# Three edits in one kernel: substitution on VectorE in the RWKV stage, new slots in the delta stage, scaled exponentials in the attentions

## The chip, the cores and the metric

One core of a Trainium2 chip runs a whole two-block network in one launch, all in 32-bit floats. The metric is the device time of one execution in microseconds, median of three.

## The reference, cut to what matters

512 tokens of width 1024 pass an RWKV-7 mixing layer, an MLP, a forgetting attention, an MLP, and then a second block: gated delta rule in both directions, latent attention (MLA), and an expert-choice MLP. Three places matter here.

```python
# RWKV-7: 16 heads of 64; the kernel works it in chunks of 64 tokens
S = S * w_t[:, :, None, :] + sa[..., :, None] * b_t[..., None, :] + v_t[..., :, None] * k_t[..., None, :]
# delta rule: 8 heads of 128, two directions, chunks of 64
t_inv = lax.linalg.triangular_solve(eye + lower, ..., left_side=True, lower=True, unit_diagonal=True)
# both attentions, in blocks of 128 queries
p = jax.nn.softmax(s, axis=-1)
return jnp.einsum('bhqk,bhkd->bhqd', p, v)
```

In both recurrences each chunk needs the inverse of a unit triangular 64x64 matrix. Both attentions need the weights p normalised, and turned, since TensorE sums over partitions.

## The kernel before, in words

**Slots and rounds.** Five engine programs are written as streams that yield at slot ends. `rounds` weaves, in each of 12 rounds, five stages of five neighbouring items: chain, scores, post, prep, fetch (this order in each slot). An item is a pair of heads `ct` in RWKV (8 items, 24 slots) and a head `hd` with both directions in delta (8 items, 32 slots). A slot fixes the order of instructions in each engine's own queue; between engines only semaphores order. So in slot n every engine does what its streams put there, and whoever is behind makes the others wait. Rounds 0 to 7 hold the projections (`pe_fetch`, four 128x512 products in slots 2, 5, 8, 11, 14 and 17 of RWKV; `pe_dfetch`, in every fourth slot of delta). Later rounds don't.

**The chain.** `pe_chain` walks eight chunks, three slots each: xs, then uu, then the new state's part `ds` and the output y. ScalarE copies xs and uu in between, VectorE adds the state (`dv_chain`, 128x64). Delta's chain has four slots per chunk.

**The inverse.** `pe_scores` makes an upward series of levels 0 to 5 with blocks of 2, 4, ... 64. Each level takes groups of 16 products of 64x64 (8 chunks, two halves; a 32-bit product is two instructions in the trace): u, then t and tt, with VectorE masking u to `A_` and copying tt to `TT`, and ScalarE copying t to `T_`. In RWKV all six levels are done so. In delta (`pe_dscores`, `dv_dscores`) levels 1 to 3 are already replaced: VectorE turns the diagonal 16x16 blocks out of the scores by 32x32 stream transposes, substitutes them column by column (`solve16`, two dependent small instructions for each j from 1 to 14), ScalarE and GpSimd spread the result back into blocks, two stream transposes return it, and TensorE does levels 4 and 5.

**The attentions.** Forgetting attention runs 40 units (8 pairs of heads, five units each, of 512 score columns in all: two whole block rows, two split 384+128, one 256+256). For a unit TensorE scores, VectorE takes the maximum (`dv_max`), ScalarE exponentiates with the sum on the side, VectorE takes the reciprocal and writes identity times reciprocal (`dv_diagonal`), TensorE multiplies each 128x128 block of exponentials by that diagonal, which turns and scales it (`pe_weights`), ScalarE copies, TensorE multiplies with the values. Unit n + 2 is scored before unit n is turned. Latent attention does the same in 16 steps of two heads (`pe_heads`, `dv_lmax`, `LDG`); in steps 0 to 2 of each four TensorE has other products between scores and weights, in step 3 they lie ahead of the scores.

In the profile almost all instructions have the line of a helper: L79 is a product, L82 a transpose on TensorE, L70 a VectorE or GpSimd operation of two tensors, L73 one with scalars, L76 the fused one, L87 a ScalarE activation.

Of the kernel before, what the change touches and what calls it, by code (L numbers as in the profile page):

```python
# [10 lines left out]
P = 128  # L11
# [130 lines left out]
def consts():  # L142
# [30 lines left out]
    for n in range(2):  # L173
        f[:, 68 + n] = np.arange(128) % 4 == np.arange(128) % 64 // 32 * 2 + n
    out["d_tri"] = np.concatenate([both(jj <= ii, jj >= ii), -1.0 * both(jj < ii, jj > ii)], axis=1)
# [45 lines left out]
def program(nc, a, out):  # L221

    ctx = ExitStack()
    with ctx:
# [31 lines left out]
        x3, h3 = kt(X[:, :]), kt(H[:, :])  # L256

# [506 lines left out]
        T_, A_ = c8(cv(512)), c8(cv(512))  # L764
# [20 lines left out]
        def bank8(b):  # L785
            return c8(BK[b][:, :])
# [193 lines left out]
        def pe_scores(pe, ct, left):  # L980
# [36 lines left out]
            pe.wait_ge(s_gp, ngp["m", ct])  # L1017
            for c in range(8):
                for h in half:
                    m = pe.mm(bank8(4)[h, c, :], m8[h, c, :], rcon("r64", rows=h), True, True)  # L1020
            m.then_inc(s_pe, npe("u", ct, 0))
# [5 lines left out]
            for lev in range(1, 6):  # L1027
                x, y = (5, 4) if lev % 2 else (4, 5)
                if lev == 1:
                    pe.wait_ge(s_dv, ndv["t", ct, 0])  # L1030
                    each(x, m8, T_).then_inc(s_pe, npe("u", ct, lev))
                yield
                if lev == 1:
                    pe.wait_ge(s_gp, ngp["tt0", ct])
                else:
                    pe.wait_ge(s_dv, ndv["tt", ct, lev - 1])
                pe.wait_ge(s_dv, ndv["a", ct, lev])
                if lev < 5:
                    each(y, TT, A_).then_inc(s_pe, npe("t", ct, lev))
                each(x, A_, TT).then_inc(s_pe, npe("tt", ct, lev))  # L1040
                yield
                for n, (src, b) in enumerate(((V, 2), (c8(KH), 2), (c8(BH), 3))):
                    if lev == 1 + n:
                        pe.wait_ge(*((s_gp, ngp["end", ct, n - 1]) if n else (s_ac, nac["v", ct])))
                        pe.wait_ge(*left[b])
                        turn(src, b).then_inc(s_pe, npe("tok", ct, n))
                        left[b] = (s_ac, nac["tok", ct, n])
                if lev < 5:
                    pe.wait_ge(s_ac, nac["t", ct, lev])
                    each(y, m8, T_).then_inc(s_pe, npe("u", ct, lev + 1))  # L1050
                yield
            yield from idle(4)

        def gp_scores(gp, ct):
# [3 lines left out]
            gp.wait_ge(s_dv, ndv["sb", ct, 1])  # L1058
            gp.tt(m8, m8, over8("r64", 0), ADD).then_inc(s_gp, ngp("m", ct))
            gp.wait_ge(s_gp, ngp.n)  # L1060
            if ct >= 2:
                gp.wait_ge(s_pe, npe["headed", ct - 2])
            gp.tt(TTs[ct % 2], m8, over8("r64", 64), MUL).then_inc(s_gp, ngp("tt0", ct))
# [6 lines left out]
            yield from idle(17)  # L1070

        def ac_scores(ac, ct):
            yield from idle(5)
            if ct >= 2:
                ac.wait_ge(s_pe, npe["headed", ct - 2])
            for lev in range(1, 6):
                yield
                if lev < 5:
                    ac.wait_ge(s_pe, npe["t", ct, lev])
                    ac.act(T_, bank8(4 if lev % 2 else 5), COPY).then_inc(s_ac, nac("t", ct, lev))  # L1080
                yield
                for n, (dst, b) in enumerate(((Vts[ct % 2], 2), (KHts[ct % 2], 2), (BHts[ct % 2], 3))):
                    if lev == 1 + n:
                        ac.wait_ge(s_pe, npe["tok", ct, n])
                        ac.act(dst, bank8(b), COPY).then_inc(s_ac, nac("tok", ct, n))
                yield
            yield from idle(4)

        def dv_scores(dv, ct):
# [13 lines left out]
            masked("sb", NRs[ct % 2], 5, 1)  # L1103
            yield
            yield
            masked("sk", AKs[ct % 2], 2, 0)
# [2587 lines left out]
```

## Time and profile before

| | us |
|---|---|
| three runs, median (lowest to highest) | 3521.67 (3516.02 to 3525.56) |
| the profiled execution | 3509.0 |
| its span, first to last instruction | 3507.2 |
| RWKV's rounds, about | 120 to 600 |
| forgetting attention's units, about | 1320 to 1430 |
| delta's rounds, about | 1905 to 2500 |
| latent attention's steps, about | 2660 to 2850 |

The tile names are: A the big arena in SBUF, SM, X, H and W other SBUF areas, con the constants, bank a PSUM bank. PE is TensorE's products, PEld its weight loads, DVE VectorE, ACT ScalarE, POOL GpSimd. "Idle before" is what the engine waited just before the instruction, and the arrow names what ended that. A run of small products on TensorE is shown with the last one's latency (0.2 to 0.3 us), so times per product are read from start to start.

### The profile page before, as it was taken

How to read it: one execution, taken by the hardware profiler on the slowest of the kernel's cores; microseconds unless marked ns; L12 is line 12 of the kernel's file. 1: busy time of each engine (PE TensorE's matmuls, PEld its weight loads, DVE VectorE, ACT ScalarE, POOL GpSimd, SP SyncE). 2: the span in 40 equal slices, each digit the busy share in tenths (PEclk: the TensorE clock that was granted, in tenths of full speed). 3: DMA queues.
4: the chain of work that ended last, by engine and by line, in shares of the span. 5: the costliest groups of instructions: out<-in, count | busy, mean ns of one | idle time of the engine just before them, and what ended most of it. 6: DMA issues, size and time to landing. Idle time of an engine off the chain costs nothing.

```text
span 3507.2 us, 51167 instructions
## 1 busy us (share of the span) xinstructions
PE 3350.6 (96%) x22310; PEld 2162.8 (62%) x22310; DVE 1580.3 (45%) x2993; ACT 761.7 (22%) x1580; POOL 379.4 (11%) x298
## 2 busy tenths in 40 slices
PE   8999998999999999999999899998999999899999
PEld 3566666888884657788887454554445656434343
DVE  4454553788743225688832666555212204201011
ACT  2323332211003025311001333233222320211111
POOL 0010110233001000122100211212100001000000
PEclk9999998999999999999999999998999999899999
DMA  5321202255651220156622111100221114699997
GB/s 198 121 74 46 87 7 78 80 180 180 204 157 61 72 77 9 49 156 187 185 84 74 48 37 26 36 25 1 58 66 43 48 44 150 248 421 421 421 421 284
DMA packets 355791, 452.81 MB, mean 129 GB/s; under 512 B 25712, under 2 KB 282992, under 8 KB 331760
## 3 DMA queue, kind: packets, MB, share of 16 engines
q1 hardware_dynamic: 355568, 449.55, 37.4%
q8 instruction: 175, 2.87, 0.3%
q14 instruction: 48, 0.39, 0.0%
HBM read 445.27 MB, written 4.20 MB: 128 GB/s over the span
## 4 chain that ended last, share of the span: by engine, by line
PE 85%; DVE 8%; DMA 3%; ACT 3%; issue 1%; POOL 0%; SPq 0%; POOLq 0%; DVEq 0%; ACTq 0%
PE bank L79 84%; DVE A L70 2%; DVE A L76 2%; DMA A<-in_w_up 2%; ACT A L87 1%; DMA W<-in_w_up 1%; DVE A L73 1%; PE bank L82 0%; POOL A L73 0%; DVE H L70 0%; ACT SM L87 0%; DVE SM L76 0%; DVE X L76 0%; DMA A<-in_x 0%; ACT H L87 0%
## 5 line engine op out<-in xcount | busy, mean ns | idle before, releaser
L79 PE MATMUL bank<-A 64*64 64x64 f32 (+6 forms) x11424 | 1004.2, 271 | 59.9 <-ACT A L87 27.8
L79 PEld LDWEIGHTS bank<-A 64*64 64x64 f32 (+3 forms) x11424 | 785.8, 152 | 322.7 <-issue 117.9
L79 PE MATMUL bank<-A,W 128*128 128x256 f32 (+1 forms) x2240 | 719.0, 475 | 2.9 <-DMA W<-in_rw_g 1.6
L79 PE MATMUL bank<-H,W 128*128 128x512 f32 (+2 forms) x1712 | 644.4, 526 | 24.8 <-ACT H L87 14.4
L79 PEld LDWEIGHTS bank<-A,W 128*128 128x128 f32 x2240 | 417.8, 191 | 253.9 <-issue 213.0
L87 ACT ACTIVATE A<-bank 128x64 f32<-128x64 f32 (+4 forms) x493 | 208.6, 427 | 1434.6 <-PE bank L79 1339.7
L79 PEld LDWEIGHTS bank<-H,W 128*128 128x128 f32 (+1 forms) x1712 | 316.5, 192 | 289.3 <-issue 257.5
L79 PE MATMUL bank<-A,H 128*64 128x512 f32 (+2 forms) x1224 | 309.6, 572 | 6.1 <-DMA A<-in_w_up 3.3
L70 DVE TENSOR_TENSOR A<-bank,A 128x256 f32<-128x256 f32 (+1 forms) x350 | 157.9, 462 | 178.1 <-PE bank L79 158.9
L70 POOL TENSOR_TENSOR A<-A 128x512 f32<-128x512 f32 (+1 forms) x103 | 145.6, 1420 | 749.6 <-ACT A L87 389.6
L87 ACT ACTIVATE A<-A 128x512 f32<-128x512 f32 (+1 forms) x238 | 138.0, 610 | 398.8 <-DVE A L70 368.5
L79 PEld LDWEIGHTS bank<-A,H 128*64 128x64 f32 (+1 forms) x1224 | 113.9, 145 | 171.6 <-issue 150.5
L79 PE MATMUL bank<-W,H 128*64 128x512 f32 (+3 forms) x952 | 208.9, 476 | 0.0
L76 DVE SCALAR_TENSOR_TENSOR SM<-W,cact,SM 128x512 f32<-128x512 f32 x206 | 188.4, 914 | 9.3
L70 DVE TENSOR_TENSOR A<-W 128x512 f32<-128x512 f32 x152 | 107.4, 747 | 176.6 <-PE bank L79 87.7
L70 DVE TENSOR_TENSOR A<-bank,SM 128x512 f32<-128x512 f32 x16 | 10.3, 686 | 344.8 <-PE bank L79 344.8
L79 PEld LDWEIGHTS bank<-W,H 128*64 128x64 f32 (+1 forms) x952 | 85.7, 159 | 101.0 <-issue 100.6
L70 DVE TENSOR_TENSOR A<-A 128x50 f32<-128x50 f32 (+9 forms) x282 | 106.5, 379 | 58.0 <-ACT A L87 49.3
L70 POOL TENSOR_TENSOR SM<-SM 128x512 f32<-128x512 f32 x31 | 41.2, 1330 | 817.5 <-ACT SM L87 815.2
L76 DVE SCALAR_TENSOR_TENSOR X<-bank,mods,X 128x256 f32<-128x256 f32 (+1 forms) x144 | 86.7, 603 | 89.7 <-PE bank L79 84.1
L79 PE MATMUL bank<-A,con 128*128 128x512 f32 (+2 forms) x174 | 92.8, 658 | 24.1 <-ACT A L87 12.2
L79 PE MATMUL bank<-H,A 128*128 128x256 f32 x448 | 107.4, 381 | 0.0
(185 smaller groups left out, 2576.5 us busy)
## 6 DMA issues: line engine op xcount, KB each, us to landing
A<-in_w_gate SPq DMA_DIRECT2D x47, 1024.0 KB, 22.4
W<-in_mod_w SPq DMA_DIRECT2D x45, 1024.0 KB, 7.3
A<-in_w_up SPq DMA_DIRECT2D x42, 1024.0 KB, 19.3
A<-in_w_down SPq DMA_DIRECT2D x35, 1024.0 KB, 27.0
W<-in_mlp_up SPq DMA_DIRECT2D x64, 512.0 KB, 5.4
W<-in_mlp_down SPq DMA_DIRECT2D x128, 256.0 KB, 4.0
W<-in_w_mod SPq DMA_DIRECT2D x24, 1024.0 KB, 5.4
W<-in_w_up SPq DMA_DIRECT2D x22, 1024.0 KB, 19.0
```

Of the source, the lines that this page charges most:

```text
L70: return self.e.tensor_tensor(o, x, y, op)
L73: return self.e.tensor_scalar(o, x, s1, s2, op0, op1) if op1 is not None else self.e.tensor_scalar(o, x, s1, None, op0)
L76: return self.e.scalar_tensor_tensor(out=o, in0=x, scalar=s, in1=y, op0=op0, op1=op1, **kw)
L79: return self.e.matmul(o, l, r, start=start, stop=stop, skip_group_check=True)
L87: return self.e.activation(o, i, func, bias=bias, scale=scale)
```

## The change

**RWKV.** The same VectorE substitution comes into `pe_scores` and its companions. TensorE's groups u0 to u3, t1 to t3 and tt1 to tt3 go; u4, t4, tt4, u5 and tt5 stay, now in slots 16, 18, 18, 19 and 21 (before 13, 15, 15, 16 and 18). VectorE adds a stream transpose in slot 1, two parity passes, a fill of ones, steps j = 1 to 14 in slots 2 to 13, and two stream transposes in slot 15, which wait for the spreads by ScalarE and GpSimd in slot 14. It drops its masks t0 and a1 to a3 and its copies tt1 to tt3. GpSimd's first TT goes, one spread comes.

**Delta.** The steps take one slot each (3 to 16; before 3 to 13, some doubled). GpSimd's spread is one masked two-tensor instruction per half (two in all, slot 17) where there were four scalar ones (slot 14); ScalarE's four stay and move from slot 14 to 17; the stream transposes move from slot 15 to 19; level 4 from slots 17 and 18 to 22 and 23, level 5 from 21 and 22 to 26 and 27. The turns of values and keys stay in slots 12, 16, 20 and 24.

**Attentions.** The diagonals go. VectorE multiplies the exponentials in place by the reciprocal, and TensorE transposes the blocks against the identity. Latent attention's `LDG` also waited for the last step's product; that wait goes.

```diff
@@ pe_scores, RWKV
-            pe.wait_ge(s_gp, ngp["m", ct])
-            for c in range(8):
-                for h in half:
-                    m = pe.mm(bank8(4)[h, c, :], m8[h, c, :], rcon("r64", rows=h), True, True)
-            m.then_inc(s_pe, npe("u", ct, 0))
...
-            for lev in range(1, 6):
+            for lev in range(4, 6):
                 x, y = (5, 4) if lev % 2 else (4, 5)
-                if lev == 1:
-                    pe.wait_ge(s_dv, ndv["t", ct, 0])
-                    each(x, m8, T_).then_inc(s_pe, npe("u", ct, lev))
+                if lev == 4:
+                    pe.wait_ge(s_gp, ngp["m", ct])
+                    pe.wait_ge(s_dv, ndv["t", ct, 3])
...
@@ gp_scores
-            gp.tt(TTs[ct % 2], m8, over8("r64", 64), MUL).then_inc(s_gp, ngp("tt0", ct))
...
+            gp.wait_ge(s_dv, ndv["inv", ct])
+            spread16(gp, AM, XI).then_inc(s_gp, ngp("ett", ct))
@@ ac_scores
+            ac.wait_ge(s_dv, ndv["inv", ct])
+            for n in range(2):
+                m = ac.act(of16(TTf)[:, :, 16 * n:16 * n + 16], XI.rearrange("p i c -> p c i"), COPY, scale=parity(n))
@@ dv_scores
+            dv.e.transpose(of16(AM), by16(NRs[ct % 2][:, :, 0, :])).then_inc(s_dv, ndv("raw", ct))
+            yield
+            dv.wait_ge(s_dv, ndv.n)
+            dv.ts(XI, of16(AM)[:, :, 0:16], parity(0), None, MUL, None).then_inc(s_dv, ndv())
+            dv.wait_ge(s_dv, ndv.n)
+            dv.stt(XI, of16(AM)[:, :, 16:32], parity(1), XI, MUL, ADD).then_inc(s_dv, ndv())
...
+            for j in range(1, 15):
+                if j not in (1, 8, 12):
+                    yield
...
+                solve16(dv, XI, XTMP, j).then_inc(s_dv, ndv() if j < 14 else ndv("inv", ct))
+            yield
+            yield
+            dv.wait_ge(s_ac, nac["et", ct])
+            dv.wait_ge(s_gp, ngp["ett", ct])
+            dv.e.transpose(by16(T_), of16(TT.rearrange("p c t -> p (c t)"))).then_inc(s_dv, ndv("t", ct, 3))
+            dv.wait_ge(s_dv, ndv.n)
+            dv.e.transpose(by16(TT), of16(AM)).then_inc(s_dv, ndv("tt", ct, 3))
@@ helper, and its use in gp_dscores
+        def spread16(e, st, x, rows=slice(0, P)):
+            n = rows.stop - rows.start
+            mask = C("iota")[rows, 68:70].unsqueeze(1).unsqueeze(3).broadcast_to([n, 16, 2, 16])
+            return e.tt(st.rearrange("p (c q j) -> p c q j", q=2, j=16), x.unsqueeze(2).broadcast_to([n, 16, 2, 16]), mask, MUL)
...
-            for n in range(2):
-                for h, i in zip(half, ("p i c -> p i c", "p i c -> p c i")):
-                    gp.wait_ge(s_gp, ngp.n)
-                    m = gp.ts(of16(DAM)[h, :, 16 * n:16 * n + 16], DXI[h, :, :].rearrange(i), parity(n, h), None, MUL, None)
+            for h, i in zip(half, ("p i c -> p i c", "p i c -> p c i")):
+                gp.wait_ge(s_gp, ngp.n)
+                m = spread16(gp, DAM[h, :], DXI[h, :, :].rearrange(i), h)
@@ dv_dscores
-                if j in (1, 3, 4, 5, 6, 7, 9, 10, 11, 12, 13):
-                    yield
+                yield
                 solve16(dv, DXI, DXTMP, j).then_inc(s_dv, ndv() if j < 14 else ndv("dinv", hd))
@@ pe_weights and dv_diagonal, forgetting attention
-                    m = pe.mm(b[:, c], Eu[n % 4][:, c], DGu[n % 4][i], True, True)
+                    m = pe.tr(b[:, c], Eu[n % 4][:, c], C("ident"))
...
-                m = dv.ts(DGu[n % 4][i], C("ident"), s[:, 4 * i + 2:4 * i + 3], None, MUL, None)
+                e = Eu[n % 4][:, o:o + 128 * qt + 128]
+                m = dv.ts(e, e, s[:, 4 * i + 2:4 * i + 3], None, MUL, None)
@@ pe_heads and dv_lmax, latent attention
-                        m = pe.mm(BK[2 + e][:, s], LE[e][:, s], LDG[e], True, True)
+                        m = pe.tr(BK[2 + e][:, s], LE[e][:, s], C("ident"))
...
-                if n:
-                    dv.wait_ge(s_pe, npe["lp", n - 1, e])
-                dv.ts(LDG[e], C("ident"), lsm[e][:, 3:4], None, MUL, None).then_inc(s_dv, ndv("ldg", n, e))
+                dv.ts(LE[e], LE[e], lsm[e][:, 3:4], None, MUL, None).then_inc(s_dv, ndv("ldg", n, e))
```

## Rows read from the trace of the kernel before

**Rows 1.** The page: span, and busy time, share and instructions by engine.
```profile
span 3507.2 us, 51167 instructions
...
PE 3350.6 (96%) x22310; PEld 2162.8 (62%) x22310; DVE 1580.3 (45%) x2993; ACT 761.7 (22%) x1580; POOL 379.4 (11%) x298
```
**Rows 2.** Busy times by stretch, RWKV: a full round, the two without projections.
```profile
core 0: us, PE busy (x) PEld busy (x) DVE busy (x) ACT busy (x) POOL busy (x), PEclk, DMA share, GB/s
430.60:491.90 61.30, 59.60 (x958) 39.96 (x955) 30.47 (x56) 19.54 (x45) 6.91 (x5) 1.00 0.14 46
491.90:533.80 41.90, 39.17 (x910) 31.52 (x908) 25.80 (x48) 17.96 (x42) 6.36 (x5) 1.00 0.02 5
533.80:567.00 33.20, 31.66 (x770) 27.25 (x768) 12.93 (x23) 9.71 (x24) 4.58 (x4) 0.95 0.10 31
```
**Rows 3.** The same for delta: a full round, the first without projections.
```profile
2226.80:2295.40 68.60, 62.20 (x509) 34.80 (x508) 40.85 (x98) 21.40 (x43) 11.59 (x10) 0.95 0.10 31
2363.80:2413.80 50.00, 38.01 (x442) 26.24 (x438) 30.96 (x84) 18.94 (x38) 7.70 (x7) 0.83 0.01 1
```
**Rows 4.** Timeline of RWKV, TensorE: start, length, then [idle before and releaser].
```profile
433.48 0.33 PE L79 MATMUL bank<-A 64*64 64x64 f32 x4
...
434.13 0.68 PE L79 MATMUL bank<-A 64*64 64x64 f32 x16 [0.32 <-ACT A L87]
...
460.67 1.10 PE L79 MATMUL bank<-W,X 64*64 64x64 f32 x32
461.60 1.57 PE L79 MATMUL bank<-A 64*64 64x64 f32 x48
```
**Rows 5.** Timeline of one full delta round, three places.
```profile
2245.34 1.27 POOL L70 TENSOR_TENSOR A<-A,con 128x512 f32<-128x512 f32 x1
2245.45 1.22 DVE L70 TENSOR_TENSOR A<-A 128x50 f32<-128x50 f32 x1
...
2253.01 0.66 PE L79 MATMUL bank<-A 128*64 128x128 f32 x8 [1.01 <-DVE A L76]
...
2259.50 4.94 POOL L73 TENSOR_SCALAR A<-A,con 64x256 f32<-64x256 f32 x4 [12.89 <-DVE A L70]
...
2264.55 1.06 DVE L2458 STREAM_TRANSPOSE A<-A 128x512 f32<-128x512 f32 x1 [3.65 <-POOL A L73]
```
**Rows 6.** Timeline of the forgetting attention (maxima), and of a latent step's weights.
```profile
1358.40 0.69 DVE L1978 TENSOR_REDUCE A<-bank 128x1 f32<-128x512 f32 x1 [0.32 <-PE bank L79]
...
1360.38 0.69 DVE L1978 TENSOR_REDUCE A<-bank 128x1 f32<-128x512 f32 x1
...
1366.80 0.76 DVE L1978 TENSOR_REDUCE A<-bank 128x1 f32<-128x384 f32 x2 [0.41 <-PE bank L79]
...
1369.30 0.75 DVE L1978 TENSOR_REDUCE A<-bank 128x1 f32<-128x256 f32 x2
...
1372.19 0.69 DVE L1978 TENSOR_REDUCE A<-bank 128x1 f32<-128x512 f32 x1 [0.32 <-PE bank L79]
...
2752.08 2.05 PE L79 MATMUL bank<-A,SM 128*128 128x128 f32 x16 [0.31 <-DVE A L73]
```
**Rows 7.** VectorE's groups by shape: busy us, mean ns, idle before.
```profile
L70 DVE TENSOR_TENSOR A<-bank,W 128x512 f32<-128x512 f32 x80 | 54.5, 684 | 47.1 <-PE bank L79 46.6
...
L2440 DVE STREAM_TRANSPOSE A<-A 128x512 f32<-128x512 f32 x8 | 8.4, 1053 | 0.3
...
L70 DVE TENSOR_TENSOR A<-A 128x56 f32<-128x56 f32 x32 | 6.9, 217 | 1.1
```
**Rows 8.** Busy times of two stretches at the start, where TensorE only transposes.
```profile
11.30:14.80 3.50, 3.46 (x17) 3.50 (x18) 0.00 (x0) 2.28 (x4) 0.00 (x0) 1.00 1.05 390
14.90:16.60 1.70, 1.70 (x17) 1.60 (x15) 0.00 (x0) 1.70 (x4) 0.00 (x0) 1.00 1.05 387
```
**Rows 9.** VectorE's scalar operations of line 73: ns min/median/max, first and last start.
```profile
L73 DVE TENSOR_SCALAR A<-con,A x96: 278/286/290, 1321.4 to 2845.3; 128x128 f32<-128x128 f32 x96
...
L73 DVE TENSOR_SCALAR A<-SM,cols x24: 476/478/1182, 1932.9 to 2350.8; 128x512 f32<-128x512 f32 x24
```

More of the change, by code:

```diff
@@ L1041, in pe_scores @@
                 yield
[L1042 to L1050, printed above, removed]
-                yield
-            yield from idle(4)
+            yield from idle(2)
         def gp_scores(gp, ct):
@@ L1069, in gp_scores @@
                 yield
-            yield from idle(17)
+            yield from idle(7)
+            gp.wait_ge(s_dv, ndv["inv", ct])
+            spread16(gp, AM, XI).then_inc(s_gp, ngp("ett", ct))
+            yield from idle(10)
         def ac_scores(ac, ct):
+            TTf = TTs[ct % 2].rearrange("p c t -> p (c t)")
             yield from idle(5)
@@ L1122, in dv_scores @@
                 yield
-            yield from idle(4)
+            yield
         def pe_chain(pe, ct):
@@ L1704, in program @@
         PTu = [HQ[:, 2048 + 512 * n:2560 + 512 * n] for n in range(4)]
-        DGu = [[cv(128) for _ in range(2)] for _ in range(4)]
         smu = [cv(8) for _ in range(4)]
@@ L2387, in pe_dscores, with tokens @@
-            yield from idle(7)
+            def tokens(n):
+                b = 1 + n % 2
+                pe.wait_ge(*left[b])
+                turn(vf if n < 2 else QK[:, :, 0, :], b, n % 2).then_inc(s_pe, npe("dtok", hd, n))
+                left[b] = (s_ac, nac["dtok", hd, n]) if n < 2 else (s_dv, ndv["dtok", hd, n])
+            yield from idle(12)
+            tokens(0)
+            yield from idle(4)
+            tokens(1)
+            yield from idle(4)
+            tokens(2)
+            yield from idle(2)
@@ new lines, in pe_dscores @@
+            pe.wait_ge(s_gp, ngp["dm", hd])
+            pe.wait_ge(s_dv, ndv["dt", hd, 3])
+            each(3, m8, DT).then_inc(s_pe, npe("du", hd, 4))
+            yield
+            pe.wait_ge(s_dv, ndv["dtt", hd, 3])
+            pe.wait_ge(s_dv, ndv["da", hd, 4])
+            each(4, TT, DA).then_inc(s_pe, npe("dt", hd, 4))
+            each(3, DA, TT).then_inc(s_pe, npe("dtt", hd, 4))
+            yield
+            tokens(3)
+            yield from idle(2)
+            pe.wait_ge(s_ac, nac["dt", hd, 4])
@@ L2488, in pe_dchain @@
+            yield
+            dv.wait_ge(s_pe, npe["dtt", hd, 5])
+            dv.e.tensor_copy(TT, bank8(4)).then_inc(s_dv, ndv("dtt", hd, 5))
+            yield from idle(5)
         def pe_dchain(pe, hd):
@@ L2719, in program @@
         QR = [cv(512) for _ in range(2)]
-        LDG = [cv(128) for _ in range(2)]
         lsm = [cv(8) for _ in range(2)]
```

198 lines of the change are left out of this document (96 added, 102 removed).

## The prediction

> **What bounds the kernel now.** I read the page first. TensorE is busy for 96% of the span, VectorE for 45%, and the granted clock in the rounds quoted below is between 0.83 and 1.00 [rows 1 to 3]. So what matters is TensorE's own work, and where it pauses. Then the busy times by stretch. One full round of the first mixing stage (RWKV; 24 slots) takes 61.3 us with TensorE busy for 59.60 and VectorE for 30.47; the two rounds without projections take 41.9 and 33.2 us [rows 2]. A full round of the delta stage (32 slots) takes 68.6 us, and its first round without projections 50.0 us at clock 0.83 [rows 3]. Last the timeline. A light slot of the RWKV chain is bare waiting: 0.32 us shown for ScalarE's copy [rows 4], and from issue to issue 0.65 us (433.48 to 434.13) where the four instructions fill 0.12, so some 0.5 us. In delta, TensorE waits 1.01 us for a state update that stands behind VectorE's queue, and VectorE itself waits 3.65 us for GpSimd's spreads [rows 5]. The forgetting attention is TensorE-bound, 1372.19 - 1358.40 = 13.79 us per pair of heads, with a second loop close behind (below) [rows 6].
>
> **Part A, RWKV.** Per pair of heads (8 of them) ten groups of 16 64x64 products go: u0 to u3, t1 to t3, tt1 to tt3. A group is 32 instructions on TensorE and takes 461.60 - 460.67 = 0.93 us [rows 4]. 10 x 0.93 x 8 = **74.4 us** of work that lies on the path.
>
> Given back, per full round:
> - Slots that lose their filler. The chain goes product, ScalarE copy, product, ScalarE copy, product, VectorE update, in slots 3c, 3c+1, 3c+2. Before, the bare slots are 1, 19, 20, 21 and 22; after, 1, 3, 6, 9, 15, 20 and 22. Two more at 0.5: **1.0 us**.
> - The end. Level 5's product moves from slot 18 to 21, where only light slots lie ahead: it waits for VectorE's masking, 0.68 us (the first row of [rows 7]), and the next round for its copy: **0.8 us**.
> - VectorE. It loses seven passes of 0.68 (t0, a1 to a3, tt1 to tt3), 4.8 us. It gains 28 substitution instructions of at most 0.217 (the smaller ones less), some 5.7 us, three stream transposes of 1.053, and two parity passes, nearest row 0.478 [rows 9]: 9.8 us ([rows 7] for the rest). Besides, a two-input VectorE instruction that meets a GpSimd one stands still: 1.22 us for one of 50 columns [rows 5], where 56 take 0.217 [rows 7]. GpSimd has five instructions per round (6.91 us) [rows 2], of which some four now meet substitution steps: 4 us. So VectorE has 30.5 - 4.8 + 9.8 + 4 = 40 us in a round of some 54: it doesn't bound, but its order shows. Bounds for what TensorE sees of it: nothing (3.4 us of projection hide every update in slots 2 to 17), or 1.01 us [rows 5] at each of 7 updates. I take **1.0**, nearer to the lower end, for that cover.
>
> - The added waits. In slot 15 VectorE waits for the spreads of slot 14. GpSimd's takes about 1.27 us (nearest row) [rows 5]; behind the wait stand t0 of the bonus and the update of slot 17, and TensorE's u4 waits for it in slot 16. Slot 14 holds 3.4 us of projection, so a full round pays **nothing**; a round without projections pays up to 1.3 us, which is in the 4 us below. In slot 14 ScalarE waits for the last substitution step; behind it stands the copy of xs, again with the projection as cover.
>
> The Trainium skill says of that standstill (SBUF — State Buffer, on the port pair that VectorE and GpSimd share) that it is an exclusive lock, held for the whole instruction. The 1.22 us agrees; the sum above goes by the row.
>
> So a full round, or one that is nearly full (six of them), gives 9.3 - 2.8 = 6.5 us: 39 us. In the two rounds without projections VectorE's 25.80 and 12.93 us [rows 2] become some 33 and 20 with many waits between, and a slot is shorter than a step and an update together; I take 4 us each, between 0 and 9.3: 8 us. A thinner TensorE there will also drop its clock more often: 0.95 now [rows 2], 0.83 in the like round of delta [rows 3], over some 60 us: between 0 and 7, I take 5. **A: 39 + 8 - 5 = 42 us**, between 20 and 68.
>
> **Part B, delta's slots.** No product goes. VectorE's steps are one per slot (before, two or three in slots 3, 8 and 13), so the update waits shrink by one step, 0.43 us, at two or three places of a round: 1.2 us in five full rounds, 6 us. GpSimd's four spreads (4.94 us) [rows 5] become two; the nearest row for one is 1.27 us, so 2.5 us, and three slots lie ahead of the wait instead of one. In a full round that wait hides behind projections; in the first one and in the first without projections it doesn't: some 3 us each, 6. The products of levels 4 and 5 leave slots 17 and 21, where they hid a ScalarE copy (two more bare, 0.5 each) for 22, 23, 26 and 27, where they hide the update (two less): nothing. The clock of 0.95 and 0.83 [rows 3] may recover a little: 3 us. **B: 15 us**, between -5 (the late levels come too late for the next round) and 28.
>
> **Part C, attentions.** 160 + 128 products of a 128x128 block by a diagonal become transposes. A product is two instructions; 16 of them take 2.05 us with the tail of the last [rows 6], some 0.11 each, so 0.22 a block. A transpose is one instruction: the same tile size has 17 in 3.50 us at the start, then 17 in 1.70 us [rows 8], at most 0.11. That saves 0.11 a block: 17.6 and 14.1 us on TensorE.
>
> VectorE now scales up to 512 columns instead of a 128-column diagonal. 128 take 0.286, 512 with a column of scalars 0.478 [rows 9]: +0.19 for one block row, about +0.15 for the split units.
> - Forgetting attention. max, exp, reciprocal, scaling, next max is a loop of its own: 1360.38 - 1358.40 = 1.98 us for a whole unit, 1369.30 - 1366.80 = 2.50 for a split one (both maxima started without a wait for TensorE) [rows 6]. Per pair of heads 2 x 2.17 + 3 x 2.65 = 12.3 us after, against TensorE's 13.79 - 20 x 0.11 = 11.6. The loop becomes the bound: 1.5 us for each of eight, less 1 for the sums of the next product that VectorE does beside the last ones: **11 us**, between 5 and 17.6.
> - Latent attention. Twelve of 16 steps have projections between scores and weights and give 0.88 each. The other four wait for the scaling already (0.31 shown) [rows 6] and give some 0.35: **12 us**, between 9 and 14.
>
> The Trainium skill (TensorE: Matmul & The Clock Gate, "Part 4: PE-mode transpose") says that a transpose doesn't count as activity for the clock gate. This trace speaks against it: 17 instructions take 3.50 us, 0.21 each, and the next 17, from 14.90 us on, 1.70 us, 0.10 each [rows 8]. That is the lower clock (1.2 GHz) and then 2.4 GHz, though the clock column, which has no record that early, says 1.00 for both, and TensorE did nothing but transposes between.
>
> **The sum.** 42 + 15 + 23 = 80 us. The profiled execution has 3509.0 us (span 3507.2), so 3429; the median of the three timed runs is 12.7 higher, so **3441.7 us**.
>
> **Rivals.**
> 1. TensorE stays the bound everywhere, and the queues hide what I deduct: 74.4 + 31.7 + 20 = 126 us, 3396. For it: 96% busy [rows 1], and VectorE below 50% in RWKV. Against: the loop of 1.98 and 2.50 us. 15%.
> 2. VectorE's order eats part of it: RWKV gives only 15 to 20 us, attention's ends stay. 3521.7 - 18 - 10 - 20 = 3474. For it: the 1.01 us in the stage that already works this way. 16%.
> 3. Slower: the state update of RWKV always stands behind a locked substitution step. Price per update 1.01 for the queue and 1.0 for the lock [rows 5], 56 updates: 112 us, of which 6 are in my sum: 3548 us. It decides from 1.5 us per update on. Against: 3.4 us of projection follow most updates before anyone needs them. 5%.
> 4. The transposes don't hold the clock. The nearest row for a stretch that drops often is 0.83 [rows 3]; over the 300 us of the two attentions that is 60 us: 3502. 2%. The page named above would have it so; [rows 8] doesn't.
> 5. The diagonal doesn't really cost two instructions, or a transpose is no cheaper in place: part C gives 0, 3465. 4%.
>
> **How the numbers follow.** My forecast has 58%. The range from 3392 to 3482 leaves out the further half of rival 1, rivals 3 and 4, and a few mishaps: under 2 in 10. Faster by over 0.3% (about 10 us, what a measurement of this kernel can tell from no change): forecast, rivals 1, 2, 4 and 5, less mishaps, 93%. Within: 3%. Slower: 4%.
>
> **What would show it.** Right: RWKV full rounds of some 54 to 55 us with VectorE near 37; 64x64 products fewer by 2560 instructions; delta's wait for GpSimd under 1 us and rounds of 67 us; maxima of the forgetting attention 2.2 and 2.65 us apart with TensorE idle for up to a tenth; latent steps shorter by 0.9. Wrong: TensorE's waits for VectorE's 128x64 updates over 1 us in RWKV, a granted clock under 0.9 there, or delta rounds longer than 69 us.

## The result and the profile after

The changed kernel takes 3468.97 us, the kernel before, timed beside it, 3523.61 (four runs each): ratio 0.985, 95% interval 0.983 to 0.987, **55 us less**. The prediction said 3441.7, with a range from 3392 to 3482. The total lies in the range, but the prediction had taken off 80 us where 55 came, and by stages it is another sum: the delta stage, put at 15 us shorter, got longer. The profiled execution takes 3460.95 us, 48 less than that of before.

The page of the changed kernel (span; busy us, share and instructions by engine). TensorE has 22310 - 19462 = 2848 instructions less: the 2560 of the RWKV products and 288 of the diagonals. VectorE has 64 us more:
```profile
span 3459.2 us, 45630 instructions
...
PE 3257.4 (94%) x19462; PEld 2062.2 (60%) x19462; DVE 1644.2 (48%) x3209; ACT 754.4 (22%) x1572; POOL 363.0 (10%) x282
```
Busy times by stretch, changed kernel (columns as in [rows 2]): two full RWKV rounds, the two rounds without projections, a full delta round and the first one without projections. They answer [rows 2, 3]:
```profile
342.70:400.10 57.40, 51.65 (x638) 31.15 (x636) 36.98 (x84) 19.00 (x44) 6.54 (x5) 1.00 0.22 67
400.10:458.40 58.30, 54.33 (x638) 32.92 (x636) 35.81 (x84) 18.88 (x44) 7.03 (x5) 0.94 0.13 42
458.40:499.70 41.30, 32.89 (x590) 23.80 (x588) 31.59 (x77) 17.22 (x41) 6.54 (x5) 0.92 0.02 6
499.70:530.00 30.30, 24.33 (x488) 19.20 (x486) 20.26 (x52) 9.50 (x25) 4.35 (x4) 0.94 0.31 101
2252.50:2321.50 69.00, 60.73 (x519) 34.54 (x519) 42.41 (x99) 21.15 (x43) 9.46 (x8) 0.98 0.07 20
2321.50:2368.50 47.00, 35.49 (x440) 23.86 (x438) 29.96 (x83) 18.87 (x38) 5.91 (x5) 0.89 0.01 2
```
A full RWKV round fell from 61.3 us to 57.4 and 58.3, not to 54 or 55. A full delta round didn't fall at all (68.1 to 68.7 us before, 68.7 to 70.7 after). The rows of before show two of its four full RWKV rounds; the other two were longer, at a lower granted clock:
```profile
240.80:304.30 63.50, 61.80 (x958) 42.04 (x956) 31.25 (x56) 19.54 (x45) 6.89 (x5) 0.96 0.15 43
304.30:369.30 65.00, 61.66 (x959) 41.77 (x958) 30.98 (x56) 19.55 (x45) 6.89 (x5) 0.97 0.18 56
```
From round to round, before: 49.1, 57.2, 63.5, 65.0, 61.3, 61.3, 41.9 and 33.2 us. Changed: 42.7, 49.9, 56.6, 58.6, 57.4, 58.3, 41.3 and 30.3. The gains are 6.4, 7.3, 6.9, 6.4, 3.9, 3.0, 0.6 and 2.9.

To follow each stage from kernel to kernel I use marks that all have: the starts of RWKV's rounds (first product of the bonus), the reciprocals of both attentions, and the first stream transpose of each delta round. The list of one line's instructions gives the ends of the last two (ns min/median/max, first and last start), here for the delta transpose, the forgetting attention's and the latent one's reciprocal. Kernel before:
```profile
L2440 DVE STREAM_TRANSPOSE A<-A x8: 1047/1052/1064, 1979.4 to 2413.8; 128x512 f32<-128x512 f32 x8
L1986 DVE RECIPROCAL A<-A x64: 142/164/166, 1321.2 to 1426.8; 128x1 f32<-128x1 f32 x64
L3060 DVE RECIPROCAL A<-A x32: 162/164/166, 2661.4 to 2845.1; 128x1 f32<-128x1 f32 x32
```
Changed kernel:
```profile
L2481 DVE STREAM_TRANSPOSE A<-A x8: 1040/1051/1065, 1934.4 to 2368.5; 128x512 f32<-128x512 f32 x8
L2031 DVE RECIPROCAL A<-A x64: 143/164/165, 1282.8 to 1384.3; 128x1 f32<-128x1 f32 x64
L3101 DVE RECIPROCAL A<-A x32: 163/164/165, 2624.6 to 2798.1; 128x1 f32<-128x1 f32 x32
```
- Up to the first reciprocal of the forgetting attention: 1321.2 - 1282.8 = 38.4 us gained (part A).
- Forgetting attention, first to last reciprocal: 105.6 to 101.5, 4.1 gained. Between it and delta another 2.5.
- Delta, from its first transpose to the latent attention's first reciprocal: 682.0 to 690.2, **8.2 lost** (part B, predicted as a gain of 15). Between the first and the last of the transposes nothing changed (434.4 and 434.1); the loss lies behind the last.
- Latent attention, first to last reciprocal: 183.7 to 173.5, 10.2 gained.

Three things stand out in the changed kernel's trace. In RWKV (TensorE; start, length, [idle before and releaser]) the bare slot is as in [rows 4], but a wait for weights is new:
```profile
425.51 0.33 PE L79 MATMUL bank<-A 64*64 64x64 f32 x4 [0.32 <-ACT A L87]
...
433.41 1.23 PE L79 MATMUL bank<-A,W 128*128 128x512 f32 x2 [1.80 <-DMA W<-in_rw_g]
```
Between 134 and 560 us TensorE waits four times for these weights, 7.2 us in all; before, once, 1.6 us. They are the gate's weights, the fifth load of a round on a ring with four slots: they get the slot of the k and r weights, which comes free at order slot 11, and are used in slot 12. By the order of the slots, the product work that stood in slots 10 to 12 had hidden part of the load, and the change took it out.

In a full delta round (TensorE and VectorE; it answers [rows 5]):
```profile
2268.92 1.27 POOL L70 TENSOR_TENSOR A<-A,con 128x512 f32<-128x512 f32 x1
2269.04 2.33 DVE L70 TENSOR_TENSOR A<-A 128x44 f32<-128x44 f32 x2
...
2275.32 0.86 PE L79 MATMUL bank<-A 64*128 64x128 f32 x8 [0.81 <-ACT A L87]
...
2277.46 1.12 PE L79 MATMUL bank<-A 128*64 128x128 f32 x8 [1.28 <-DVE A L76]
...
2287.99 3.71 POOL L70 TENSOR_TENSOR A<-A,con 64x512 f32<-64x512 f32 x3 [15.33 <-DVE A L70]
...
2294.51 1.05 DVE L2497 STREAM_TRANSPOSE A<-A 128x512 f32<-128x512 f32 x1 [0.29 <-ACT A L87]
...
2299.20 1.79 PE L79 MATMUL bank<-A 64*128 64x128 f32 x40 [0.38 <-ACT A L87]
2301.78 2.67 PE L79 MATMUL bank<-A 64*64 64x64 f32 x72 [0.79 <-DVE A L70]
...
2309.69 1.79 PE L79 MATMUL bank<-A 64*128 64x128 f32 x40 [0.38 <-ACT A L87]
2312.28 1.74 PE L79 MATMUL bank<-A 64*64 64x64 f32 x40 [0.79 <-DVE A L70]
```
VectorE's wait for the spreads did go (3.65 to 0.29 us), but nobody on TensorE was waiting for it. Instead levels 4 and 5 have moved to where ScalarE's copy and VectorE's masking of u lie open, 0.38 and 0.79 twice each.

Still, what the five rounds from the second to the sixth lost (5.6 us), the first (50.2 to 47.2) and the first without projections (50.0 to 47.1) gave back. The stage's net loss is in the round after these, the second without projections (cut at TensorE's 32 products `bank<-con,A 64*128 64x64`, early in each round). Before, then changed:
```profile
2414.38:2474.71 60.33, 56.43 (x467) 29.23 (x465) 24.85 (x75) 14.15 (x30) 27.80 (x21) 0.94 0.01 1
```
```profile
2369.13:2437.95 68.82, 59.65 (x467) 30.64 (x465) 27.50 (x75) 14.26 (x30) 26.16 (x19) 0.90 0.00 1
```
TensorE's shown waits there are 9.2 us instead of 4.0. GpSimd's long run of other work on X, which stood behind the spreads (from 2445.3 us, 31 us into the round), now starts at 2371.0, 2 us into it, beside VectorE's first steps: two of VectorE's parity passes take 2.31 us together instead of 1.16, and a wait of TensorE for VectorE right after is 2.6 instead of 0.8. A wait of 2.3 for a ScalarE copy, which stands behind the four moved spreads, is new. The granted clock is 0.90 instead of 0.94.

### The profile page after: what moved, and what is told of

Same layout as the page of the kernel before. It is cut to its first block, busy times and chain, and to the rows that moved or that the text cites. A ratio compares the mean times of both kernels' runs of the same rounds, so it can differ in the third digit from the quotient of the medians.

```text
span 3459.2 us, 45630 instructions
## 1 busy us (share of the span) xinstructions
PE 3257.4 (94%) x19462; PEld 2062.2 (60%) x19462; DVE 1644.2 (48%) x3209; ACT 754.4 (22%) x1572; POOL 363.0 (10%) x282
## 4 chain that ended last, share of the span: by engine, by line
PE 82%; DVE 9%; ACT 4%; DMA 4%; issue 1%; SPq 0%; POOLq 0%; POOL 0%; DVEq 0%; ACTq 0%
PE bank L79 82%; DVE A L70 2%; DMA A<-in_w_up 2%; DVE A L76 2%; ACT A L87 2%; DVE A L73 1%; PE bank L82 1%; ACT A L86 1%; DMA W<-in_w_up 1%; DVE A L2023 1%; DMA W<-in_mod_w 1%; DVE H L70 0%; ACT SM L87 0%; DVE X L76 0%; DMA A<-in_x 0%
## 5 line engine op out<-in xcount | busy, mean ns | idle before, releaser
L79 PE MATMUL bank<-A 64*64 64x64 f32 (+6 forms) x8800 | 904.3, 286 | 97.9 <-ACT A L87 49.9
L79 PEld LDWEIGHTS bank<-A 64*64 64x64 f32 (+3 forms) x8800 | 684.4, 156 | 365.2 <-issue 99.2
L87 ACT ACTIVATE A<-bank 128x512 f32<-128x512 f32 (+4 forms) x469 | 193.8, 418 | 1377.9 <-PE bank L79 1333.4
L70 DVE TENSOR_TENSOR A<-A 128x14 f32<-128x14 f32 (+9 forms) x506 | 160.9, 320 | 65.7 <-ACT A L87 49.2
L79 PE MATMUL bank<-A,con 128*128 128x512 f32 (+2 forms) x174 | 88.8, 634 | 22.0 <-ACT A L87 12.3
```

Source lines behind the costliest of these rows:

```text
L70: return self.e.tensor_tensor(o, x, y, op)
L79: return self.e.matmul(o, l, r, start=start, stop=stop, skip_group_check=True)
L87: return self.e.activation(o, i, func, bias=bias, scale=scale)
```

## The experiments

Every kernel was timed beside the kernel before on its own chip; ratios are to that, with 95% intervals.

### One part at a time

**RWKV alone.** The kernel before with this and the rest of the first mixing stage's part of the diff:
```diff
-            for lev in range(1, 6):
+            for lev in range(4, 6):
```


> The RWKV part of the change alone (the substitution on VectorE in the first mixing stage), with delta rounds and attentions as before. Theory, from the round starts of the two traces: 38 us shorter than before, about 3484 us, with the delta stage's first to last stream transpose at 467 us and the time between reciprocals in the forgetting attention at 105.6 us, both as before. The prediction on record gave this part 42 us (3480). Rival, that the parts help or hurt one another through what they prefetch across the stage borders: the sum of the three parts alone differs from 54.6 us by more than 5.

3472.31 us against 3518.56, ratio 0.987 (0.986 to 0.988): **46 us** shorter; its round starts run from 140.3 to 503.9, 363.6 us where before has 399.3. The other two kernels that keep the old RWKV take 401.8 and 405.1, so the profiled execution of before stood at the low end, and the part may be worth more than the 38 read first. The prediction's 42 lies at the edge of the timed interval (42 to 51).

**Delta alone.**
```diff
-                if j in (1, 3, 4, 5, 6, 7, 9, 10, 11, 12, 13):
-                    yield
+                yield
                 solve16(dv, DXI, DXTMP, j)...
```


> The new slots of the delta rounds alone. Theory, from the two traces: 7 to 8 us longer than before, about 3530 us, with rounds that have projections of 69 to 70 us instead of 68.3. The prediction on record: 15 us shorter, 3508, rounds of 67. Rival: the slots are worth nothing by themselves and what the trace of after showed is one execution's scatter, within 3 us of before.

3530.10 against 3518.56, ratio 1.0034 (1.0022 to 1.0046): **12 us longer**. First transpose to the latent attention's first reciprocal: 691.8 us against 682.0; the second round without projections takes 67.6 us (60.3 before). The sign of part B was wrong, by itself as well as inside the change.

**Attentions alone.**
```diff
-                    m = pe.mm(b[:, c], Eu[n % 4][:, c], DGu[n % 4][i], True, True)
+                    m = pe.tr(b[:, c], Eu[n % 4][:, c], C("ident"))
```


> The attentions' part alone (exponentials scaled on VectorE, then turned). Theory, from the two traces: forgetting attention 6.6 us and latent attention 10.2 us shorter, 17 us together, about 3506 us. The prediction on record: 11 and 12, 23 us, 3500. Rival, that the forgetting attention gains nothing and the latent one all that is seen: 10 us.

3501.53, ratio 0.9956 (0.994 to 0.997): 17 us shorter. The trace has 2.7 us of it in the forgetting attention (105.6 to 102.9) and 10.0 in the latent one. Its profiled execution was the longest of the seven (3514.6), so only the stage lengths are read from it, not its total; where the other 4 us lie isn't shown.

**The change without its delta part** (all slots and spreads of the delta rounds as before):

```diff
 # against the changed kernel
             for j in range(1, 15):
-                yield
+                if j in (1, 3, 4, 5, 6, 7, 9, 10, 11, 12, 13):
+                    yield
```


> The change without its delta part: delta rounds as before, RWKV and attentions as changed. Theory: the delta part costs 7 to 8 us inside the change, so this runs 62 us under before, about 3461 us, and beats the changed kernel by 7. The prediction on record, by which the delta part saves 15 us: 40 us under before, about 3484. Rival, no effect of the delta part: 55 us under before, 3469.

3461.88, ratio 0.9836 (0.982 to 0.985), 57 us shorter: so less than 46 + 17, by some 7. Against the changed kernel's 0.985 (0.986 in a repetition below) it is 5 to 9 us ahead, though the intervals meet. The single parts are nearly, not exactly, additive.

### What costs delta its sign

**Levels one slot earlier.** Products, ScalarE copy and VectorE maskings of levels 4 and 5 move from slots 22, 23, 26, 27 to 21, 22, 25, 26, the same places between the chain's products as the old 17, 18, 21, 22:
```diff
             tokens(2)
-            yield from idle(2)
+            yield
             pe.wait_ge(s_gp, ngp["dm", hd])
...
-            yield
+            yield from idle(2)
             tokens(3)
-            yield from idle(2)
+            yield
             pe.wait_ge(s_ac, nac["dt", hd, 4])
```


> The changed kernel with the delta rounds' levels 4 and 5 one slot earlier, so that their products stand again in the same places between the chain's products as before the change, and everything else of the new slots kept (substitution one step per slot, one spread instruction per half, spreads at slot 17). Theory, that the places of the levels cost the delta part its sign (two more bare waits for ScalarE of 0.5 us and two maskings of 0.8 in the open per full round): rounds with projections fall from 69.5 to 67.5 us, first to last stream transpose from 474 to about 462, the whole about 12 under the changed kernel, 3458. Rival, that the substitution's new order and its meeting with GpSimd's masking cost it: the rounds stay at 69 or more, 3469.

3450.92 against 3516.59, ratio 0.982 (0.980 to 0.984). Delta to the latent attention: 2622.1 - 1945.5 = 676.6 us, 13.6 under the changed kernel and 5.4 under before. Full rounds are 66.3 to 68.2 us (68.7 to 70.7 in the changed kernel). The end of such a round, TensorE: where the changed kernel has four waits between 2299 and 2318, this one has none until the next copy:
```profile
2297.92 0.66 PE L79 MATMUL bank<-A 128*64 128x128 f32 x8 [0.34 <-DVE A L76]
2298.41 1.04 PE L79 MATMUL bank<-con,A 128*64 128x128 f32 x16
2299.38 3.70 PE L79 MATMUL bank<-H,W 128*128 128x512 f32 x8
2303.01 4.83 PE L79 MATMUL bank<-A 64*64 64x128 f32 x116
2307.67 1.04 PE L79 MATMUL bank<-con,A 128*64 128x128 f32 x16
2308.64 3.70 PE L79 MATMUL bank<-H,W 128*128 128x512 f32 x8
2312.27 3.90 PE L79 MATMUL bank<-A 64*64 64x128 f32 x84
```
All that was changed here is the place of two levels, so the place costs the stage some 13 us, more than it lost in all. It isn't the only loss: the second round without projections still takes 67.9 us here (60.3 before).

**The cheaper spread alone**, on the change without the delta part:
```diff
-            for n in range(2):
-                for h, i in zip(half, ("p i c -> p i c", "p i c -> p c i")):
-                    m = gp.ts(of16(DAM)[h, :, 16 * n:16 * n + 16], DXI[h, :, :].rearrange(i), parity(n, h), ...)
+            for h, i in zip(half, ("p i c -> p i c", "p i c -> p c i")):
+                m = spread16(gp, DAM[h, :], DXI[h, :, :].rearrange(i), h)
```


> RWKV and attentions as changed; the delta rounds keep their old slots and get only the new spread on GpSimd, one instruction for each half instead of two. Theory, that VectorE's wait for GpSimd's spreads (over 3 us a round before) is worth something by itself: 1 us per full round, first to last stream transpose from 466 to 460, the whole 6 under the kernel without the delta part (3456). Rival, that this wait lies beside TensorE's work: within 2 us of it.

3453.11, ratio 0.982 (0.980 to 0.984) against 0.9836 (0.982 to 0.985) without it: some 6 us by the medians, with intervals that overlap, but the traces have less than 2 of it in this stage. Delta to the latent attention: 679.2 us against 680.9. Full rounds stay at 68.3 and 69.3, the first round at 50.2; what is gained lies in the first round without projections (51.3 to 48.4), and half of it is lost again in the next (57.2 to 58.8). The wait of 3.65 us lay beside TensorE's work in full rounds, as the prediction had said.

### What bounds the RWKV rounds now

**Gate weights beside the value weights.** The value weights fill half a ring slot. The gate's 256 columns go into the other half, and need no slot of their own:
```diff
-            load(sp, ("rv", ct), (0, (0, P), (8, 128), rows128(a["rw_wv"][:, cs])))
+            load(sp, ("rv", ct), (0, (0, P), (8, 128), rows128(a["rw_wv"][:, cs])), *post)
...
-                if r >= 4:
+                if r >= 8:
                     sp_post(sp, r - 4)
```


> The changed kernel with the gate weights of the RWKV rounds (256 columns) loaded into the free half of the slot that the value weights take, instead of a slot of their own that comes free only one slot of the order before they are used. Theory, that the weight supply took back a part of the gain (TensorE waits 1.8 us for these weights in four rounds): 7 us shorter in RWKV, round starts 57 instead of 58.3 apart, the whole 7 to 9 under the changed kernel. Rival, that TensorE then waits as long for something else in the same place: no difference.

Twice the expected gain in the stage: first to last round start 350.8 us instead of 364.8. Busy times by stretch of this kernel, four full rounds:
```profile
229.50:283.90 54.40, 51.27 (x638) 30.99 (x635) 35.55 (x84) 18.88 (x44) 6.55 (x5) 1.00 0.23 70
283.90:338.40 54.50, 51.38 (x642) 31.09 (x639) 35.65 (x84) 18.89 (x44) 6.54 (x5) 1.00 0.24 71
338.40:392.80 54.40, 51.28 (x638) 31.00 (x636) 35.55 (x84) 18.89 (x44) 6.54 (x5) 1.00 0.23 71
392.80:447.30 54.50, 51.38 (x642) 31.09 (x639) 35.66 (x84) 18.89 (x44) 6.55 (x5) 1.00 0.09 27
```
Rounds of 54.4 and 54.5 us, all at a granted clock of 1.00, where the changed kernel has 56.6, 58.6, 57.4 and 58.3 in the same four, two of them at 0.94. The sum over the four falls by 13.1 us: 7.2 are the waits, and the two rounds at 0.94 have 54.3 and 54.5 us of TensorE busy where the others have 51.7, 5.5 us together. So some two fifths of the gain are the clock, which no longer falls. In the changed kernel all four rounds have the wait (1.74, 1.94, 1.74 and 1.80 us, ending at 261.1, 317.5, 377.1 and 433.4), and only behind the second and the fourth is the clock low:
```profile
319.00:321.00 2.00, 2.00 (x4) 0.50 (x6) 0.00 (x0) 0.00 (x0) 0.00 (x0) 0.50 0.00 0
377.00:380.00 3.00, 2.91 (x30) 1.40 (x32) 0.00 (x0) 0.22 (x1) 0.00 (x0) 1.00 0.00 0
```
Why two and not four isn't shown; without the waits it is none. The Trainium skill (TensorE: Matmul & The Clock Gate, "HAM oscillation — how this bites in real kernels") describes the like in a kernel whose waits for weights are 3 to 5 us: the work behind each of them starts at the lower clock. The traces here agree for two of four waits, of under 2 us.

The whole kernel took 3458.07 us, ratio 0.984 (0.983 to 0.986), 3 to 8 us ahead of the changed kernel's two ratios, with intervals that overlap. The forgetting-attention kernel on the same chip (next), which has the old loads, took 3466.03 although it gains some 6 us in its own stage.

### What bounds the forgetting attention

**Less scaling.** Only the first 128 columns of each row block are scaled; the scaling of the other exponentials is left out.
```diff
-                e = Eu[n % 4][:, o:o + 128 * qt + 128]
+                e = Eu[n % 4][:, o:o + 128]
```


> The changed kernel, but the forgetting attention scales only the first 128 columns of each row block of exponentials on VectorE; the scaling of the others is left out. Theory, that the loop of maxima, exponentials, reciprocals and scaling bounds this stage: 0.2 us less for each single maximum and each double one, six steps per pair of heads, so pairs 11.6 us apart instead of 12.55 where TensorE's own work then bounds it, 6 us less in all. Rival, that TensorE or its clock bounds it already: reciprocals first to last stay at 101.5 us.

This kernel leaves out a part of the attention's own work, so it only measures. First to last reciprocal 97.3 us, where the kernels on this chip with the whole scaling have 103.2 and 103.3: the expected 6. But a pair of heads still takes 12.2 us, not 11.6. Of 12.55 only 0.35 went; the other part is the first pair (13.7 to 12.2) and the step in the middle (16.9 to 14.9), where the clock no longer fell. VectorE's loop bounds the pairs in part, but at 12.2 something else than TensorE's bare work takes over. That wasn't followed further.

What the clock does there shows in the busy times of the changed kernel in short stretches around the first pair:
```profile
1288.00:1290.00 2.00, 0.66 (x4) 0.42 (x4) 0.91 (x5) 1.09 (x5) 0.00 (x0) 1.00 0.01 4
1290.00:1291.00 1.00, 0.53 (x10) 0.53 (x12) 0.96 (x5) 0.42 (x1) 0.00 (x0) 1.00 0.00 0
1291.00:1292.00 1.00, 1.00 (x13) 0.67 (x7) 0.50 (x2) 0.47 (x3) 0.00 (x0) 0.52 0.00 0
1292.00:1293.00 1.00, 1.00 (x2) 0.49 (x3) 0.38 (x3) 1.00 (x5) 0.00 (x0) 0.50 0.00 0
1293.00:1294.00 1.00, 1.00 (x4) 0.48 (x3) 0.46 (x2) 0.04 (x1) 0.00 (x0) 0.50 0.00 0
```
TensorE is busy for 0.66 of 2 us and 0.53 of the next one, and then the granted clock is 0.50, the lower of the two levels (1.2 of 2.4 GHz), for three microseconds, in which 13, 2 and 4 matmuls start. In the kernel before, the least busy three microseconds at this stage's start have TensorE at 1.96, and the clock is 1.00 throughout.

### Both repairs, on one chip with the changed kernel

**The changed kernel again**, no edit:

> The changed kernel unchanged, on the same chip as the three kernels beside it, so that they can be compared with it directly. Expected 0.985 of before, 3462 to 3469 us; RWKV from first to last round start 365 us, delta from first to last stream transpose 474 to 477.

3471.53, ratio 0.986 (0.984 to 0.988); RWKV 364.9 us. The changed kernel repeats.

**Both repairs**, the diffs of the levels and of the gate weights together:

> The changed kernel with both repairs: levels 4 and 5 of the delta rounds one slot earlier, and the RWKV gate weights in the free half of the value weights' slot. Theory, that the two losses are independent: RWKV 14 us shorter (351 between the first and last round start), delta 11 to 13 us shorter (463), 25 us under the changed kernel, about 3440 us, 0.978 of before. Rival, that one gives back what the other gains (the clock falls as TensorE waits less evenly, or scatter between chips made them look large): less than 18 us under the changed kernel.

3446.15, ratio 0.979 (0.977 to 0.981): **25 us under the changed kernel** on the same chip, as expected, 71 under before. RWKV 350.8 us, delta to the latent attention 672.4. Between RWKV and the forgetting attention it gives back 4 us (783 to 787); that wasn't followed.

**The gate weights' repair with delta's old slots and the new spread**, the diffs of the two kernels above together:

> As the kernel with both repairs, but the delta rounds in their old slots with only the new spread of GpSimd. Theory, that of the whole delta part only the cheaper spread and the early first steps are worth anything and the slots of the substitution are not: within 3 us of the kernel with both repairs. Rival, that the one-step-per-slot order has a worth of its own once the levels stand right: 5 us or more behind it.

3450.38, ratio 0.980 (0.978 to 0.983). 4 us behind, with intervals that overlap widely: whether the one-step-per-slot order is worth anything stays open; it is at most a few us (672.4 against 678.8 in the profiled executions, which differ in clock too). The traces split it: between the first and the last transpose the new order with its levels one slot earlier takes 420.5 us and the old one 432.8, but the second round without projections takes 64.7 against 58.8. The kernel with levels one slot earlier against the one with the spread alone shows the same: 421.5 against 433.2, and 67.9 against 58.8. What the order gains before, it gives back by half or more there.

**With fillers in the forgetting attention.**
```diff
                     pe_weights(pe, n)
+                    if n in (0, 1, 2, 3, 20, 21, 22, 23):
+                        for k in range(8):
+                            pe.tr(BK[5][:, 128 * (k % 4):128 * (k % 4) + 128], C("ident"), C("ident"))
```


> As the kernel with both repairs, with eight extra transposes of a constant block into an unused bank after the weights of units 0 to 3 and 20 to 23 of the forgetting attention, where the changed kernel's TensorE had waited 1.5 us and its granted clock was then 0.50 for some 3 us (1291 to 1294). Theory, that the waits made the clock fall: with the filling TensorE keeps 1.00, the first pair of heads takes 12.6 us instead of 13.7, and the 16.9 between units 20 and 25 becomes 15.3; 7 us of fillers lie in the waits; 1 to 3 us shorter. Rival, that the fillers only add their own time (0.9 us each set) because they stand ahead of the waiting copy's consumer: up to 4 us longer.

3441.86, ratio 0.978 (0.976 to 0.980): 4 us under the kernel without them, with overlapping intervals. The traces tell more. Busy times of the whole forgetting attention, first the kernel with both repairs, then the one with fillers also:
```profile
1272.00:1378.00 106.00, 94.11 (x690) 70.58 (x689) 66.97 (x202) 54.84 (x163) 0.00 (x0) 0.97 0.03 7
```
```profile
1270.00:1376.00 106.00, 97.91 (x762) 76.15 (x764) 68.46 (x208) 55.46 (x164) 0.00 (x0) 1.00 0.03 9
```
The clock stays at 1.00; the first pair takes 12.7 us instead of 13.7, as expected. The step in the middle takes 16.4 instead of 16.9, not 15.3: there the fillers' own 0.9 us per set stand in the way. First to last reciprocal 101.8 instead of 103.3. So work that computes nothing kept the clock up and took 1.0 us off the first pair, which is 13.5 to 13.7 in all nine traces that have this change's attentions and no fillers. For the stage as a whole a gain isn't shown: in six of the nine it takes 103.2 or 103.3, in one 102.9, but 101.5 in both executions of the changed kernel, whose clock didn't fall in the middle. The Trainium skill (TensorE: Matmul & The Clock Gate, "Part 4: PE-mode transpose") has transposes not count as activity for the clock; here the fillers are transposes and nothing else, and the clock stayed at 1.00. By its median this is the fastest kernel here, 75 us (2.2%) under before.

## Why the prediction was right and wrong

**RWKV, 42 predicted: 38 in the profiled execution, 46 timed. Right in sum, not in its parts.** The products cost what was said: with the weight supply mended, full rounds are 54.4 us, the prediction's "54 to 55", with VectorE at 35.6 to 37 (predicted 37 in its signs, 40 in its sum), and the bare slots cost 0.3 shown each, as [rows 4]. In the kernel as it is, terms were missing or mis-sized:
- The supply of weights. A round that shrinks meets its loads earlier. The prediction asked what VectorE and ScalarE would be late with and never asked it of SP's queue. Cost: 7.2 us of waiting and 5.5 of clock over four rounds.
- The clock. I took 5 us, over the last rounds only. Those rounds run at 0.92 and 0.94 (before 1.00 and 0.95), but full rounds fell to 0.94 too.
- The two rounds without projections gave 0.6 and 2.9 us, not 4 each: VectorE's busy time rose from 25.8 to 31.6 us in one of 41.3, among waits, which was said, but priced too low.
- Against these, the full rounds of before weren't all 61.3 us: two took 63.5 and 65.0, with a granted clock of 0.96 and 0.97 and, in one of them, a wait of 1.6 us for the same weights. So the first six rounds still gave 33.9 us of the 39, and the last two 3.5 of 8. That before had a part of these losses already, which the prediction didn't know, brought the sum near. It is luck.

The waits for VectorE's updates, rival 3, didn't come: TensorE waits 6.3 us in 8 places for such updates in the whole stage, 0.8 each in the mean, and none of these is in a round with projections, where the prediction had put 1.0 us a round.

**Delta, 15 predicted as a gain: 8 lost, 12 when timed alone. Wrong in sign.** The step that failed is "the products of levels 4 and 5 leave slots 17 and 21 ... for 22, 23, 26 and 27, where they hide the update (two less): nothing". Listed by TensorE's shown waits in one full round: before 2.25 + 0.38 + 1.01 + 0.38 + 0.99 + 0.16 + 0.38 + 0.34 + 0.38 = 6.3 us. Changed: 1.79 + 0.81 + 1.28 + 5 x 0.38 + 2 x 0.34 + 2 x 0.79 = 8.0. Levels one slot earlier: 1.79 + 0.82 + 1.28 + 3 x 0.38 + 2 x 0.34 = 5.7. The updates that the levels were to hide they had hidden before as well: t and tt stand between the chain's product that starts an update and the one that needs it at the old place and at the new one (0 and 0.16 us shown before, 0 after). So "two less" was nothing. The two bare copies came as said (0.38 each), and masking u, which the move put next to its user with nothing between, costs 0.79 twice. The prediction counted which copies lose cover and forgot the moved work's own dependency. By the first-to-last transposes the whole place costs 434.1 - 421.5 = 12.6 us. Three more terms:
- The second round without projections, 60.3 to 68.8 us, 8.5 lost, stands in no term of the sum. With levels one slot earlier it stays at 67.9. The eight traces with the new slots have 64.7 to 68.8 there, the six with the old ones 57.2 to 60.3. That GpSimd's work and ScalarE's spreads at their new places cause it is read from the timeline, not tested.
- Update waits "shrink by one step, 0.43 us, at two or three places": in the round listed they shrink from 2.5 to 2.0 us in all. One place less shows a wait, but the one of 1.01 has grown to 1.28. Just before it, two substitution steps stand locked for 2.33 us (1.47 before), because GpSimd's next instruction (1.04 us), which before stood behind the spreads, now follows its masking at once. That this is what lengthens the wait is argued, not tested.
- The spreads: 3 us each in two rounds. The first round gained 2.9 us (50.2 to 47.2) and the first without projections 2.9 (50.0 to 47.1). The size is right. But the cheaper instruction alone gave the first round nothing (50.4 to 50.2), so there the gain is from the new slots, and the delta part alone left the other round at 49.8, so that gain isn't certain.

**Forgetting attention, 11 predicted: 4.** The loop was sized right. Timeline of VectorE's maxima, changed kernel, which answers [rows 6]:
```profile
1309.10 0.68 DVE L2023 TENSOR_REDUCE A<-bank 128x1 f32<-128x512 f32 x1
1311.65 0.76 DVE L2023 TENSOR_REDUCE A<-bank 128x1 f32<-128x384 f32 x2 [0.34 <-PE bank L79]
1314.28 0.75 DVE L2023 TENSOR_REDUCE A<-bank 128x1 f32<-128x384 f32 x2
1316.90 0.75 DVE L2023 TENSOR_REDUCE A<-bank 128x1 f32<-128x256 f32 x2
1319.53 0.68 DVE L2023 TENSOR_REDUCE A<-bank 128x1 f32<-128x512 f32 x1
1321.66 0.68 DVE L2023 TENSOR_REDUCE A<-bank 128x1 f32<-128x512 f32 x1
```
A single one takes 1321.66 - 1319.53 = 2.13 us (predicted 2.17), a split one 1316.90 - 1314.28 = 2.62 (2.65), a pair of heads 1321.66 - 1309.10 = 12.56 (12.3). What failed is the factor, and the bare 1.5 us per pair was 1.2. Before, pairs were 12.7, 13.8, 13.7, 13.8, 15.4, 12.7 and 13.7 us apart; I had read one of 13.79 and multiplied by eight. Changed, they are 13.6, 12.6, 12.5, 12.6, 15.3, 12.5 and 12.6: four gain 1.1 to 1.2, two gain 0.1 and 0.2, and the first loses 0.9, most of it to the clock (13.7 becomes 12.7 where fillers keep it up).

**Latent attention, 12 predicted: 10.2.** From reciprocal to reciprocal, the steps with projections gave 0.8 to 1.0 us each, and three of the other four 0.4 each (7.1 to 6.7), as said. The first of these four lost 1.0 (7.1 to 8.1): behind a wait of 2.5 us, where before has 2.3, the granted clock is 0.58 and then 0.50 for some 3.6 us, and before it is 1.00. In the other three the wait for the scaling grew, from 0.31 [rows 6] to 0.51 (TensorE, changed kernel; the transposes of the step are in the same row):
```profile
2710.64 1.45 PE L82 MATMUL bank<-con,SM 128*128 128x128 f32 x8 [0.51 <-DVE SM L73]
```

**The rivals.** Rival 1 (TensorE bound everywhere) is out: its busy share fell to 94%. Rival 2 (VectorE's order eats part) is in its size nearest (3474), but not in its parts: RWKV gave 38 and not 15 to 20, and what took from it was first the weights and the clock. Rival 4 (transposes don't hold the clock) as a rule for the attentions is out: a stage full of them ran at 1.00 from 1296 to 1386 us, and in the kernel with fillers the added transposes are what kept it up. Rival 5 is out by the attentions' kernel.

## What to carry to other kernels

When a round gets shorter, go through every queue that feeds it and ask how late each load starts: a ring with one slot too few shows nothing until the work that covered it is gone. Work moved in a hand-written order carries its own waits with it: check what stands between it and its user at the new place, and keep its phase in the dependent chain. And multiply a per-step gain only after reading all the steps, not one: the rounds that the rows of before left out held a part of RWKV's gain and the whole net loss of delta.

## What the runs showed of the hardware

- Here the lower clock came in the work behind a pause. Removing waits of 1.8 us brought 3.3 us per round, because two of four rounds had lost 2.7 us of TensorE time at the lower clock.
- Sixty-four transposes of a constant into an unused bank (x762 against x690 matmuls recorded in the stage) took the stage's granted clock from 0.97 to 1.00, and its first pair of heads from 13.7 to 12.7 us.
- A VectorE two-input instruction locked out by GpSimd isn't merely slowed: two that take some 0.2 us each [rows 7] took 2.33 beside GpSimd's 1.27 and 1.04, and ended when the second of these did (2271.37 and 2271.31 us).
